# A hybrid decoder layer: expert units of 32 tokens, eleven 2 MB weight slots, attention in another order

## The reference

```
mod = silu(c) W_ada + b_ada -> shift1, scale1, gate1, shift2, scale2, gate2
h1  = RMSNorm(x) * (1 + scale1) + shift1
u   = h1 @ W_in                       # conv-GLU | q | k | v | branch gates
conv branch: GLU -> causal depthwise conv, width 31 -> LayerNorm -> swish -> W_conv_out
attn branch: differential attention, 8 heads, QK norm, partial rotary -> RMSNorm -> W_attn_out
x   = x + gate1 * ((sigmoid(g_conv) * y_conv + sigmoid(g_attn) * y_attn) @ W_o)
h2  = RMSNorm(x) * (1 + scale2) + shift2
logits = h2 @ w_router + b_router ; top 4 of 32 experts, softmax over the four
for e in 32 experts:                  # w_up[e] 1024 x 2048, w_down[e] 1024 x 1024
    gu  = h2 @ w_up[e] + b_up[e]
    act = min(glu, 7) * sigmoid(1.702 * glu) * (clip(lin, -7, 7) + 1)    # glu, lin: even, odd columns of gu
    y  += combine[:, e] * (act @ w_down[e] + b_down[e])
x   = x + gate2 * y
```

## Time and profile before

| | us |
|---|---|
| median of 3 runs | 1405.62 |
| lowest and highest | 1401.92, 1407.08 |
| profiled execution, its own time | 1405.55 |
| span of the profiled execution | 1403.8 |
| PE busy | 1278.8 (91%) |
| DVE busy | 391.9 (28%) |
| ACT busy | 217.4 (15%) |
| POOL busy | 59.9 (4%) |
| moved by DMA | 477.28 MB, mean 340 GB/s |

### The profile page before, as it was taken

One profiled execution on the slowest core, in us unless ns is written; L12 is line 12 of the kernel. 1 busy time (PEld: TensorE's weight loads), 2 busy tenths in 40 slices (PEclk: granted clock), 3 DMA queues, 4 the chain that ended last, 5 costly groups with the idle time before them and its releaser, 6 DMA issues.

```text
span 1403.8 us, 19151 instructions
## 1 busy us (share of the span) xinstructions
PE 1278.8 (91%) x6945; PEld 520.9 (37%) x6946; DVE 391.9 (28%) x1054; ACT 217.4 (15%) x452; POOL 59.9 (4%) x83
## 2 busy tenths in 40 slices
PE   2899999999979999899898889999998889999997
PEld 0683444444443333233232223333332222333332
DVE  0499937541341111211111121112111111112111
ACT  1100122540121111111111111111111111111111
POOL 2100000025320000000000000000000000000000
PEclk7999999999969999999999999999999999999999
DMA  9939591346439999999999999899999999899997
GB/s 314 346 123 379 217 362 60 120 121 186 144 124 339 409 410 410 410 409 410 410 409 410 410 409 410 319 406 409 410 410 410 409 410 410 327 399 410 410 409 302
DMA packets 133791, 477.28 MB, mean 340 GB/s; under 512 B 9752, under 2 KB 9785, under 8 KB 130698
## 3 DMA queue, kind: packets, MB, share of 16 engines
q1 hardware_dynamic: 129636, 472.15, 86.5%
q0 software_dynamic: 1200, 3.28, 0.9%
q10 hardware_dynamic: 2934, 1.58, 0.4%
HBM read 473.83 MB, written 1.05 MB: 338 GB/s over the span
## 4 chain that ended last, share of the span: by engine, by line
PE 45%; SPq 31%; DMA 16%; issue 4%; ACT 2%; DVE 1%; DVEq 0%
SPq L390 26%; PE bank L1141 13%; DMA weights<-in_w_up 13%; PE bank L1371 12%; PE bank L1387 6%; PE bank L1131 4%; DMA weights<-in_w_in 3%; PE bank L1263 2%; PE bank L1346 2%; PE bank L1338 1%; SPq L418 1%; SPq L419 1%; SPq L420 1%; SPq L421 1%; SPq L417 1%
## 5 line engine op out<-in xcount | busy, mean ns | idle before, releaser
L1371 PE MATMUL bank<-weights,buf_d 128*64 128x512 f32 x2176 | 505.0, 601 | 49.0 <-DMA weights<-in_w_up 49.0
L1371 PEld LDWEIGHTS bank<-weights,buf_d 128*64 128x64 f32 x2176 | 145.0, 137 | 381.0 <-issue 243.7
L1387 PE MATMUL bank<-weights,buf_d 128*64 128x512 f32 x1088 | 246.7, 595 | 0.0
L1141 PE MATMUL bank<-weights,buf_d 128*128 128x512 f32 x320 | 139.2, 593 | 1.1 <-DMA weights<-in_w_in 1.1
L1387 PEld LDWEIGHTS bank<-weights,buf_d 128*64 128x64 f32 x1088 | 74.1, 136 | 125.6 <-issue 117.9
L1067 DVE TENSOR_SCALAR u_conv<-bank 128x256 f32<-128x256 f32 x68 | 28.6, 421 | 247.4 <-PE bank L1371 247.4
L803 DVE SCALAR_TENSOR_TENSOR weights<-u_conv,convw,weights 128x256 f32<-128x256 f32 x240 | 96.9, 480 | 0.3
L1060 DVE TENSOR_SCALAR u_conv<-iota_s,u_conv 128x128 f32<-128x128 f32 x68 | 20.5, 344 | 270.5 <-PE bank L1371 270.5
L677 ACT COPY buf_d<-bank 128x256 f32<-128x256 f32 x68 | 25.3, 373 | 418.8 <-PE bank L1397 418.8
L1141 PEld LDWEIGHTS bank<-weights,buf_d 128*128 128x128 f32 x320 | 60.7, 190 | 74.8 <-issue 72.6
L681 ACT ACTIVATE u_conv<-u_conv 128x256 f32<-128x256 f32 x34 | 14.2, 416 | 385.9 <-DVE u_conv L1067 385.9
(11 more groups left out here) (290 smaller groups left out, 828.4 us busy)
## 6 DMA issues: line engine op xcount, KB each, us to landing
weights<-in_w_up SPq DMA_DIRECT2D x256, 1024.0 KB, 18.0
weights<-in_w_down SPq DMA_DIRECT2D x128, 1024.0 KB, 18.3
weights<-in_w_in SPq DMA_DIRECT2D x14, 2048.0 KB, 18.3
weights<-in_w_ada SPq DMA_DIRECT2D x12, 2048.0 KB, 18.8
weights<-in_w_conv_out SPq DMA_DIRECT2D x2, 2048.0 KB, 11.5
weights<-in_w_attn_out SPq DMA_DIRECT2D x2, 2048.0 KB, 8.3
weights<-in_w_o SPq DMA_DIRECT2D x2, 2048.0 KB, 10.9
qkT<-modrow POOLq DMA_DIRECT2D x16, 128.0 KB, 3.9
```

The source lines that it names most:

```text
L1141: ins = t.matmul(bank(use)[:, :], lhsT[:, k, P * tt:P * tt + P], blk(n)[:, k, :], start=(k == 0 and bias is None), stop=(k == KD - 1))
L1371: ins = t.matmul(UP[a][SLOTS * i:SLOTS * i + SLOTS, :], xgT[:, k, :], wslot(slot, spare_at)[:, k % 2, NB * i:NB * i + NB], start=False, st ...
L1387: ins = t.matmul(DOWN[SLOTS * i:SLOTS * i + SLOTS, :], actT[:, a, k % 2, SLOTS * (k // 2):SLOTS * (k // 2) + SLOTS], wslot(slot)[:, k % 2, ...
```

## The change

- `SLOTS` is 32: a unit has 32 tokens, four column groups of the PE array work at once, on four quarters of 512 columns of `w_up`. An expert with `n` tokens gets max(1, ceil(n / 32)) units.
- The loop over units becomes 32 loops in a row, one for each expert, with the expert's slots fixed in the code. They run from `begin` to `end`, the latter read from `unit_ends`.
- An expert is 6 chunks of 2 MB: four of `w_up` (256 whole rows; a partition takes two neighbouring rows, 16 KB in one run) and two of `w_down` (512 rows; two runs of 8 KB for each partition). They go round 11 slots. Six are the ring places; the other five lie over the memory of first-stage buffers (gates; v and k; qkT; conv sums and x; small constants), whose contents stay until their last reader. What the expert loop needs then lives in `buf_c`, `buf_d`, `u_conv` and `late`.
- SP loads ten chunks (expert 0, and 0 to 3 of expert 1) at points of the first stages and the router, the eleventh after `units_ready`.
- The gather multiplies `h2` in fp32 with `pick` (8 matmuls of 256 columns), gives token rows, and ACT copies them; PE transposes them in two. The bf16 split on POOL goes, with ACT's cast.
- `down` sums the even and the odd rows in separate column groups, and `combine` adds both.
- In attention, the masks of both halves come first, then equal query blocks of both halves side by side; the transposes of `pa` (`turn`) come in the middle of the next head's gate projection.
- POOL's work on the expert biases waits for `swish_ready` in place of the `oT` transposes; DVE waits for it before `gate2`.

```diff
-SLOTS = 64
+SLOTS = 32
-NSLOT = 12
-SLOTF = 2 * D
-SPARE = 3
+NSLOT = 11
+GATE_SLOT, VALUE_SLOT, HEAD_SLOT, X_SLOT, SMALL_SLOT = 6, 7, 8, 9, 10
+SLOT_ORDER = (0, VALUE_SLOT, 1, 2, 3, GATE_SLOT, 4, 5, HEAD_SLOT, X_SLOT, SMALL_SLOT)
...
+            def load_chunk(e, j):
+                if j < 4:
+                    src = w_up[0, e, 2 * P * j:2 * P * j + 2 * P, :].rearrange("(p r) n -> p (r n)", r=2)
+                    dst = wslot(e, j)
+                else:
+                    src = w_down[0, e, NB * (j - 4):NB * (j - 4) + NB, :].rearrange("(g p r) n -> p g (r n)", g=2, r=2)
+                    dst = wslot(e, j).rearrange("p (g n) -> p g n", g=2)
+                sp.dma_start(dst, src).then_inc(w_full[chunk_slot(e, j)], 16)
+            sp.wait_ge(*used[COUT0])
+            load_chunk(0, 0)
+            full(sp, OT_USE + 3)
+            load_chunk(0, 1)
+            sp.wait_ge(*used[COUT0 + 1])
+            load_chunk(0, 2)
+            for i in range(2):
+                sp.wait_ge(*used[AOUT0 + i])
+                load_chunk(0, 3 + i)
+            full(sp, MT_USE + 3)
+            load_chunk(0, 5)
+            for i in range(2):
+                sp.wait_ge(*used[WO0 + i])
+                load_chunk(1, i)
+            sp.wait_ge(gate2_ready, 2)
+            load_chunk(1, 2)
+            full(sp, H2T_USE[3])
+            load_chunk(1, 3)
+            sp.wait_ge(units_ready, 2)
+            load_chunk(1, 4)
+            for e in range(EXPERTS - 1):
+                end = sp.value_load(unit_ends[0:1, e:e + 1], min_val=e + 1, max_val=UCOLS - 1)
+                for j in range(CHUNKS):
+                    n = CHUNKS * e + j + NSLOT
+                    if n < CHUNKS * EXPERTS:
+                        sp.wait_ge(chunk_used[j], end)
+                        load_chunk(n // CHUNKS, n % CHUNKS)
...
+                for part in range(2):
+                    t.matmul(PS[4 + 2 * par + part][:, 0:384], identb[:], maskb[:], start=True, stop=False)
+                for blk_q, (a, b) in enumerate(((0, P), (P, 3 * P))):
+                    for part in range(2):
+                        rows = slice(HD * part, HD * part + HD)
+                        ins = t.matmul(PS[4 + 2 * par + part][:, a:b], qT[rows, h, P * blk_q:P * blk_q + P], kT[rows, h, 0:b - a],
+                                       start=False, stop=(blk_q == 1))
...
+                for k in range(KD):
+                    if h and k == KD // 2:
+                        turn(h - 1)
+                    ins = t.matmul(bank(gate_use(h))[:, :], h1T[:, k, P * par:P * par + P], blk(n)[:, k, :],
+                                   start=False, stop=(k == KD - 1))
...
+            def unit(e, u):
+                pe.wait_ge(xc_ready, u + 1)
+                pe.wait_ge(sel_ready, u + 1)
+                bias_rows(UP, range(GROUPS), 0)
+                for j in range(4):
+                    w = up_chunk(e, j)
+                    pe.wait_ge(w_full[chunk_slot(e, j)], chunk_landed(e, j))
+                    for r in range(2):
+                        for g in range(GROUPS):
+                            ins = t.matmul(UP[SLOTS * g:SLOTS * g + SLOTS, :], xgT[:, r, SLOTS * j:SLOTS * j + SLOTS],
+                                           w[:, r, NB * g:NB * g + NB], start=False, stop=(j == 3 and r == 1))
+                    ins.then_inc(chunk_used[j], 1)
+                pe.wait_ge(oe_ready, u + 1)
+                combine()
+                bias_rows(DOWN, (0, 2), 2 * D)
+                pe.wait_ge(pick_ready, u + 2)
+                gather()
+                pe.wait_ge(act_ready, u + 1)
+                transpose_halves(TR, 0, act).then_inc(t_done, 1)
+                pe.wait_ge(xs_ready, u + 2)
+                transpose_halves(GX, T, xg)
+                pe.wait_ge(pickw_ready, u + 1)
+                for tt in range(TT):
+                    ins = t.transpose(GX[:, P * tt:P * tt + P], pickw[:, tt, :], ident[:])
+                ins.then_inc(xt_done, 1)
+                pe.wait_ge(actT_ready, u + 1)
+                for h in range(2):
+                    w = down_chunk(e, h)
+                    pe.wait_ge(w_full[chunk_slot(e, 4 + h)], chunk_landed(e, 4 + h))
+                    for g in range(2):
+                        at = SLOTS * (2 * h + g)
+                        for i in range(2):
+                            for r in range(2):
+                                rows = slice(SLOTS * (2 * i + r), SLOTS * (2 * i + r) + SLOTS)
+                                ins = t.matmul(DOWN[rows, :], actT[:, r, at:at + SLOTS], w[:, g, r, NB * i:NB * i + NB],
+                                               start=(r == 1 and h == 0 and g == 0), stop=(h == 1 and g == 1))
+                    ins.then_inc(chunk_used[4 + h], 1)
+            begin = 0
+            for e in range(EXPERTS):
+                end = pe.value_load(unit_ends[0:1, e:e + 1], min_val=e + 1, max_val=UCOLS - 1)
+                with pe.Fori(begin, end) as u:
+                    unit(e, u)
+                begin = end
```

More of the change, by code:

```diff
@@ L85, in build, with small @@
         u_conv = sb("u_conv", [P, KD, PAD + T])
[L86 to L90, removed]
+        late = sb("late", [P, 3 * D // 2])
+        ident = sb("ident", [P, P])
+        unit_ends = sb("unit_ends", [1, EXPERTS], I32)
+        gates = slot(GATE_SLOT).rearrange("p (t n) -> p t n", t=TT)
+        v_tok = slot(VALUE_SLOT, 0, 2 * D).rearrange("p (t d) -> p t d", t=TT)
+        buf_k = slot(VALUE_SLOT, 2 * D).rearrange("p (t d) -> p t d", t=TT)
+        qkT = slot(HEAD_SLOT).rearrange("p (a h t) -> p a h t", a=2, h=HEADS)
+        conv_acc = slot(X_SLOT, 0, 2 * D).rearrange("p (k t) -> p k t", k=KD)
+        x_tok = slot(X_SLOT, 2 * D).rearrange("p (t d) -> p t d", t=TT)
+        carved = 0
+        def small(shape, dt=F32):
+            nonlocal carved
+            size = math.prod(shape[1:])
+            width = (size + 1) // 2 if dt == BF16 else size
+            flat = W[0:shape[0], BLOCKF * SMALL_SLOT + carved:BLOCKF * SMALL_SLOT + carved + width]
+            carved += width
+            assert carved <= BLOCKF
+            flat = flat if dt == F32 else flat.bitcast(dt)
+            if len(shape) == 2:
+                return flat
+            names = "abc"[:len(shape) - 1]
+            return flat.rearrange(f"p ({' '.join(names)}) -> p {' '.join(names)}", **dict(zip(names, shape[1:])))
         h1, q_tok = buf_c, buf_c
@@ L131, in build @@
[L131 to L140, removed]
+        Cmb = area_q[:, 0:T]
@@ L141, in build @@
+        upos = area_k[:, 1360:1488].rearrange("p (t u) -> p t u", t=TT)
+        uwt = area_k[:, 1488:1616].rearrange("p (t u) -> p t u", t=TT)
+        gate2 = area_k[:, 1616:1616 + NB]
+        ebias = late[0:3 * EXPERTS, :].bitcast(BF16)
+        ebias_f, ebias_r = area_k[0:3 * EXPERTS, 0:D], area_k[0:3 * EXPERTS, D:2 * D]
+        modrow2 = late[:, 0:2 * NB].rearrange("p (a n) -> p a n", a=2)
         modrow = modrow2[:, 0, :]
+        qk_junk = small([P, T])
         bias_f = v_tok[0:96, 0, 0:NB]
-        bias_b = sb("bias_b", [96, NB], BF16)
@@ L183, in build @@
[L183 to L189, removed]
-        unit_i = sb("unit_i", [1, 3 * UCOLS + 2], I32)
-        unit_spare = sb("unit_spare", [1, UCOLS], I32)
@@ L205, in build @@
         w_full = [sem(f"w_full{i}") for i in range(NSLOT)]
-        w_free = sem("w_free")
+        chunk_used = [sem(f"chunk{j}_used") for j in range(CHUNKS)]
         in_c, in_x, in_rows, in_cols, in_small, in_bias, in_norm2, in_moe, in_rowsb, in_eb, in_rows2 = (
```

440 lines of the change are left out of this document (164 added, 276 removed).

## The result

The changed kernel takes 1333.13 us (median of 4 runs, 1331.90 to 1334.07) against 1405.69 before (4 runs, 1401.92 to 1407.08): a ratio of 0.949, interval 0.947 to 0.950. It is 72.6 us faster; the forecast was 62.6 us faster, 1343. The profiled execution took 1331.9 us for a span of 1330.0.

What follows compares the result with a forecast made beforehand. The prediction took the DMA weight stream as the bound: loads from 407.4, 901.6 us for 181 chunks, stalls to 1325.8, clock 3 and end 12.6 give span 1341.4, forecast 1343 us; range 1322 to 1358, 8 in 10 from 1318 to 1385.

Steps and rivals of the forecast that it cites:

- the head start of expert 1: Before the expert loop: ten chunks loaded ahead, the eleventh once tables are ready; cost to other loads taken as 0.
- attention: First stages: paired score matmuls and the earlier turn save 10 us; bounds -13 and +4.
- The router's part: Between attention and loop: dropping the bf16 split and small steps saves 4 us; bounds -6 and 0.
- Rate: Weight stream: larger packets lift 410 GB/s to 421, 4.98 us a chunk; bounds 410 and 427.
- Start: Loop's beginning: first unit at 403.4 us, the first chunk's slot loading again at 407.4.
- PE's unit: Expert loop: a 32-token unit takes PE 15.6 us, bounds 15.1 and 18.1; 47 units stay under the stream's time.
- rival B: Experts of several units: PE bound with units of 18.1 us, +30 us, 1373; chance 0.12.
- Stalls: Slot ring: only expert 25's four units stall the stream, 12.8 us, and the double experts behind it add 4.
- Clock: Expert loop: PE falls to 1.2 GHz in single-unit experts, costing 3 us at expert 25 and a 12.6 us end.
- A: Weight stream: larger packets bring nothing, 410 GB/s holds; 1364 us; chance 0.15.
- C: Expert loop: PE at 1.2 GHz decides, slower than before, from a mean unit of 19.6 us; chance 0.05 slower.
- D: Before the loop: attention stays as long and five extra chunks land late; 1353 to 1363 us; chance 0.12.

Runs made afterwards that it cites:

- the six gathers: Changed kernel with each unit's gather issued six times over, same result, so a unit of PE work becomes 19.3 us: 1393.52 us, ratio 0.992.
- the imitation: Changed kernel with 34 units as if of 64 tokens, every up and down matmul issued twice, tokens beyond 32 left out: 1329.59 us, ratio 0.947.

## Why the prediction was right, step by step

**The gain and its parts.** Undone one at a time: packets 37.2 us, the head start of expert 1 16.6, attention 11.8. The router's part was not undone; from the traces below it is 3.5, and that POOL's split was its largest piece is argued. These are 69.1 of 72.6. Parts undone one at a time needn't add up, and what makes the rest isn't shown. It is not the stalls. Before, the dips of the earlier trace rows, 319 and 406, 327 and 399, lose some 16 us against 410; after, the one dip and what follows it lose 17. What the traces do show beside the four parts: the start of the loop, 242 GB/s over 23 us, runs at 429 after, and the last down half takes 1.9 us in place of 3.6. Each of the four was forecast as a mechanism, and each is there.

**Rate: the term that was mis-sized.** The forecast took 421 GB/s for all, 4.98 us a chunk, and kept 427 as a bound. Up to the dip the stream ran at 425: 379.6 MB in 893 us in place of 902, 8 us of the 10 by which the forecast was too high. The value chosen was the nearest size measured; the fixed cost per packet that the three sizes of the earlier trace rows gave was the better guide, and the runs at 8 KB and 16 KB show it: 421 and 428. With 16 KB in four chunks of six, the mean of 421 and 427 was to be had from the same rows.
The ceiling of 435 GB/s that the Trainium skill gives ("DMA: Bandwidth & Descriptors", "Where 436 GB/s comes from") was not reached by any size; 428 over 100 us is the most. That section also lets some 358 GB/s bind a transfer from HBM to SBUF, which it reckons as a stack's 716 GB/s shared by two cores; here, with one core at work, the plateau is 67 to 70 above.

**Start.** The first gather came at 399.39 (forecast "near 400"; 414.00 in the earlier trace rows), the first up matmul at 403.39 (forecast 403.4; 417.83 before). Timelines of the kernel after, with PE's first head's scores, the end of attention, the router's step, and the loop's start:
```profile
216.45 0.49 PE L1179 MATMUL bank<-weights 128*128 128x384 bf16 x2
...
217.73 0.39 PE L1190 MATMUL bank<-weights 96*128 96x512 bf16 x1
...
288.93 0.38 PE L1116 MATMUL bank<-weights 96*128 96x512 bf16 x1
...
388.87 0.17 DVE L960 TENSOR_TENSOR weights<-weights 128x8 f32<-128x8 f32 x1
...
399.39 1.93 PE L1321 MATMUL bank<-buf_c,u_conv 128*32 128x256 f32 x16 [1.10 <-DVE u_conv L1016]
...
403.39 1.94 PE L1359 MATMUL bank<-weights,buf_d 128*32 128x512 f32 x8
...
408.77 9.95 SPq L404 DMA_DIRECT2D weights<-in_w_up  x4
```
And of the kernel before, the end of attention:
```profile
300.06 0.38 PE L1139 MATMUL bank<-bias_b,bsel 96*128 96x512 bf16 x1
```
The score stretch is 217.73 - 216.45 = 1.3 us (2.22 in the earlier trace rows, forecast 1.35). The matmul that follows the attention began at 300.06 before and begins at 288.93: 11.1, where 10 were forecast. The way from there to the gather is 3.5 shorter (14.6 less 11.1; forecast 4), and L960 takes 0.17 us where L963 took 1.71. The threshold steps of the router are seven, not the six of the forecast (three before), which costs it 0.2 us.
One thing was missing. The next load of the first chunk's slot stands at 408.77, not 407.4. The forecast gave the first chunk's matmuls 2.0 us, which is the full clock; but PE was at 0.50 of its clock as they began (402 to 404), as the earlier trace rows could have warned with 0.78 and 0.80 on both sides of the loop's start, and the first unit's up took 8.51 us in place of 6.87. DMA stood still meanwhile, 0 GB/s at 406 to 408. By the 225 GB/s of 408 to 410 the bytes flow from 408.9 on, 1.5 us later than forecast.

**PE's unit.** 15.0 us, in the first unit's successors as in the doubles. The steps had summed to 15.2; the 0.4 added for the loop is not to be seen, nor is any gap where one expert's code ends and the next begins (rival B). The instruction queue's load grew from 12 to 45 packets at no visible cost.

**Stalls.** One dip, at 1145 to 1165, from expert 25; none at 15. 1145 to 1165 us at a mean of 97 GB/s are 15.4 lost against 425, and 421 behind it another 1.4: 16.8. The forecast had 12.8 + 4. The sum is the same by luck: the dip was 2.6 deeper, and the doubles behind it cost less. Leaving out the fourth unit takes 14 away.

**Clock: right that it falls, wrong that it costs.** Single experts have the pacing that the forecast named. Timeline of PE in two of them, kernel after, and the window of such a stretch:
```profile
480.23 1.92 PE L1359 MATMUL bank<-weights,buf_d 128*32 128x512 f32 x16 [2.75 <-DMA weights<-in_w_up]
485.12 3.51 PE L1359 MATMUL bank<-weights,buf_d 128*32 128x512 f32 x16 [2.98 <-DMA weights<-in_w_up]
...
509.76 3.32 PE L1359 MATMUL bank<-weights,buf_d 128*32 128x512 f32 x16 [2.75 <-DMA weights<-in_w_up]
...
539.24 3.02 PE L1359 MATMUL bank<-weights,buf_d 128*32 128x512 f32 x16 [2.74 <-DMA weights<-in_w_up]
```
```profile
436.00:560.00 124.00, 86.92 (x612) 23.41 (x606) 15.35 (x48) 12.54 (x21) 0.00 (x0) 0.85 1.01 425
```
A chunk's matmuls take 1.92 us at 2.4 GHz and about 3.5 at 1.2 GHz, with some in between; the mean is 0.85, not the steady 0.50 of the earlier trace rows. At 3.5 us they still end before the next landing, and from 509.76 to 539.24 an expert takes 29.5, which is the stream's pace. The Trainium skill ("TensorE: Matmul & The Clock Gate", "Loop structure matters more than you think") calls a loop with a long DMA wait before every matmul the bad one; with waits of 3 us the trace agrees that the clock falls, in part of the bursts, and shows no time that it cost in the loop. The 1.6 us of the first unit came behind the router, before this pacing began.
The forecast also read the earlier trace rows wrongly. It took 20 to 30 us as blocks 5 us apart. The timeline of PE there, kernel before, has one block only, behind 13.8 us without any:
```profile
27.57 3.44 PE L1097 MATMUL bank<-weights,c_act 128*32 128x512 f32 x16 [13.76 <-DMA weights<-in_w_ada]
```
So that row showed the clock after a long idle stretch, and not the pacing of the new loop.
The forecast had put +3 behind it at expert 25, and half clock at the end. Neither came. The end:
```profile
1320.78 1.92 PE L1386 MATMUL bank<-weights,buf_d 128*32 128x512 f32 x16
1322.78 0.69 DVE L1057 TENSOR_TENSOR buf_d<-bank,u_conv 128x512 f32<-128x512 f32 x1 [4.85 <-PE bank L1386]
1323.61 1.99 PE L1334 MATMUL bank<-buf_d 64*128 64x512 f32 x8 [0.90 <-DVE buf_d L1057]
```
The last down half takes 1.92 us and not 3.5, combine 1.99 and not 3.8: 9.2 us from 1320.78 to the end of the span, 3.4 under the forecast's 12.6. That and the 3 at expert 25 are the second wrong term. A small one was left out: the stream's last bytes move at 1319.3 (131 GB/s in the window from 1319), and the matmuls on them begin 1.5 us later.

**The sum again.** Forecast span 1341.4; start +1.5, rate -8, clock at 25 -3, end -3.4, last landing +1.5: 1330.0, as measured. The rate is read to 0.5 GB/s, 1 us, so the last digit means nothing.

**The rivals.** A fell with the plateau at 425. Its price was too low: 1364 was forecast for it, and the 4 KB run took 1370; to the 8 KB run that is 29.5 us, where the forecast had 24 less 3. B and C fell with the unit of 15.0, and the six gathers put C's point near where it was expected. D fell with the first gather at 399.

## What to carry to other kernels

Where a stream of weights sets the pace, look first at the run that each descriptor moves, before buffers and order: here the step from 4 KB to 16 and 8 KB was half of the gain, and three sizes already in the trace foretold it. Count a weight ring's depth against the longest time that one expert holds its slots, and use idle DMA time ahead of the loop for its next loads: here five chunks landed early were worth 16.6 us. PE work that ends before the next landing is free at either clock, and so was its grain: units of 32 and, by the imitation, of 64 came out within 4 us. That holds as long as the experts of several units find slack in the ring: 4.3 us more a unit cost 60 us. And look at what stands before a row of the trace, not only at the row: the clock of 0.50 belonged to an idle stretch.

## What the runs showed of the hardware

- Rate of a stream of loads from HBM on this one core, by length of a run: 2 KB 387 GB/s, 4 KB 409, 8 KB 421, 16 KB 428. The loads are of 2 MB, those of 4 KB runs of 1 MB. In time for 1,000 bytes the steps are 0.139, 0.070 and 0.039 ns, each half the one before it, as a fixed cost per packet would make them.
- TensorE's clock didn't settle at 1.2 GHz with 5 us between bursts in the loop (0.85, bursts of 1.92 and 3.5 us in turn), though it did at 20 to 30 us of the span, where PE had stood still for 13.8 us. What keeps it up between the bursts of the loop wasn't tested.
- A DVE operation on 8 elements a partition took 1.71 us in the router while POOL ran a product of 2.12 us, and 0.17 in the kernel after, where POOL is idle there. That POOL was the cause is argued from this pair only; no run put POOL's work back.
- 32 experts' code in a row, in place of one loop body, raised instruction loads from 0.20 to 0.74 MB and showed no wait.
